# The last layer norm of a two-layer decoder: the first row tile's normalisation is given to ScalarE and GpSimd

## The chip, the cores and the metric

The kernel runs on one core of a Trainium2 chip. The core has five engines that run their own instruction streams and meet at semaphores: TensorE (PE, matmuls), VectorE (DVE), ScalarE (ACT), GpSimd (POOL) and SyncE (SP, which here only issues DMAs). The metric is the device time of one execution in microseconds, lower is better.

## The reference

A decoder of two layers over 256 tokens with 1024 features. The first layer has sparse attention and a dense SwiGLU, the second sliding-window attention and a top-2-of-8 mixture of experts. Each half layer ends in a layer norm, four in all. The change touches the last one alone:

```python
def layer_norm(x, g, b):
    xf = x.astype(jnp.float32)
    mu = xf.mean(-1, keepdims=True)
    var = jnp.square(xf - mu).mean(-1, keepdims=True)
    return ((xf - mu) * lax.rsqrt(var + LN_EPS) * g + b).astype(x.dtype)
...
            ffn = moe_swiglu(h, moe_router[l // 2], moe_w_in[l // 2], moe_w_out[l // 2])
        h = layer_norm(ALPHA * h + ffn, ln_g[l, 1], ln_b[l, 1])
...
    return h
```

## The kernel before

The 256 tokens are two row tiles `tt` of 128 tokens, one token to a partition. `h[:, tt, :]` and `pre[:, tt, :]` hold 1024 columns of each in SBUF, and `lnp[:, 0, :]` and `lnp[:, 1, :]` the norm's gain g and bias b, copied to all partitions.

Some 1,320 us of the program come ahead of the last norm: projections, attention, the dense layer, and the experts, whose weights are streamed from HBM while TensorE multiplies. After the last expert, TensorE's `put_back` adds the experts' rows to what already stands in PSUM (`bank[4 * tt + j]`, 256 columns each, `j` from 0 to 3), first for tile 0, then for tile 1, and raises `e_back` after each of the eight pieces. From there on, the order on each engine is the order in which the code is written, and engines wait for each other by counting semaphores:

- VectorE, for a tile: four `bn_stats`, one a bank; `center`, which merges them (`bn_aggr`, mean and variance in `mv`), adds epsilon (`var_ready`), and writes `pre = (bank - mean) * g` in four pieces; then the inverse of the root. Tile 0 is done whole, up to the inverse (`root_inverted`), before the statistics of tile 1. For tile 1, `scale` writes `h = pre * inverse + b` in two halves (`h_ready`).
- ScalarE: the square root for tile 0 (`root(0)`), then `pre * inverse` of tile 0 in two halves (`pre_scaled`), then `root(1)`, for which VectorE waits in `scale`.
- GpSimd: adds the bias to each half of tile 0 (`first_scaled`). These are its last two instructions.
- SyncE stores the four halves of the output, 256 KB each, in a fixed order on one queue: tile 0's first and second half, then tile 1's. A store that has to wait holds the ones behind it. The program ends when all four have landed:

```python
            for n in range(4):
                if n < 2:
                    sp.wait_ge(first_scaled, n + 1)
                else:
                    sp.wait_ge(h_ready, 12 + n - 1)
                tt, cols = n // 2, slice(512 * (n % 2), 512 * (n % 2) + 512)
                sp.dma_start(out[0, tt * P:tt * P + P, cols], h[:, tt, cols]).then_inc(done, 16)
            sp.wait_ge(done, 16 * 4)
```

`step(...)` issues an instruction and has the engine wait for its end before the next one; `chained(...)` only counts it.

Of the kernel before, what the change touches and what calls it, by code (L numbers as in the profile page):

```python
# [10 lines left out]
ALU = mybir.AluOpType  # L11
ACT = mybir.ActivationFunctionType
X = mybir.AxisListType.X

P = 128
# [144 lines left out]
def decoder_kernel(nc, x, positions, w_in_a, w_out_a, cmp_pos, cmp_w1, cmp_w2, w_kv_shared, w_q_b, w_out_b,  # L160
                   sinks_b, ln_g, ln_b, dense_w_in, dense_w_out, moe_router, moe_w_in, moe_w_out, out):
    ctx = ExitStack()
    with ctx:
        def sb(name, shape, dt=F32):
            return ctx.enter_context(nc.sbuf_tensor(name, shape, dt))

        def sem(name):
            return ctx.enter_context(nc.semaphore(name))
# [34 lines left out]
        sums = sb("sums", [P, 4, 4])  # L203
# [3 lines left out]
        stats = sb("stats", [P, NT, 4, 6])  # L207
        mv = sb("mv", [P, NT, 2])
        std = sb("std", [P, NT, 2])
        lg = sb("lg", [P, 8, NT, NE])  # L210
        selb = sb("selb", [P, NT, NE], BF16)
        top = sb("top", [P, 12, NT, 1])
# [17 lines left out]
        def place(*parts):  # L230

            size = 0
            found = []
            for name, shape, dt in parts:
                found.append(nc.alloc_sbuf_tensor_at(name, shape, dt, offset=base[0]))
                n = 4
                for x_ in shape[1:]:
                    n *= x_
                size = max(size, n)
            base[0] += size  # L240
            return found if len(found) > 1 else found[0]
# [6 lines left out]
        pre = place(("pre", [P, NT, D], F32))  # L248

        lnp, cmp_x = place(("lnp", [P, 2, D], F32), ("cmp_x", [P, 2, CMP_PAIRS, 64], F32))  # L250
# [54 lines left out]
        bank = [psum[:, i, :] for i in range(8)]  # L305
# [18 lines left out]
        dve_step = sem("dve_step")  # L324
# [76 lines left out]
        e_added = sem("e_added")  # L401
        root_inverted = sem("root_inverted")
        pre_scaled = sem("pre_scaled")
        first_scaled = sem("first_scaled")
        done = sem("done")
        zeros_ready = sem("zeros_ready")
# [238 lines left out]
        def _(pool):  # L645
# [98 lines left out]
                                            bass.IndirectOffsetOnAxis(ap=there_i[:, k, tt, :], axis=0)).then_inc(found, 16)  # L744
            for q in range(2):
                cols = slice(512 * q, 512 * q + 512)
                pool.wait_ge(pre_scaled, q + 1)
                pool.tensor_tensor(h[:, 0, cols], pre[:, 0, cols], lnp[:, 1, cols], ALU.add).then_inc(first_scaled, 1)


# [1 line left out]
        def _(act_e):  # L752
            def load_norm(k):
                for part, src in enumerate((ln_g, ln_b)):
                    act_e.dma_start(lnp[:, part, :], src[k // 2, k % 2:k % 2 + 1, :].to_broadcast([P, D]))\
                         .then_inc(ln_landed, 16)
# [3 lines left out]
            def split_weights(upto):  # L760

                upto = min(upto, N_FIRST)
                for n in range(n_round[0], upto):
                    if whole(n):
                        continue
                    act_e.wait_ge(landed[n % RING], 32 * (n // RING + 1))
                    if n >= SPLITS:
                        act_e.wait_ge(used, halves_last(n) + 1)
                    size = size_of(n)
                    act_e.activation(wh[:, n % SPLITS, 0:size], slot_of(n)[:, 0:size], ACT.Copy).then_inc(rounded, 1)  # L770
                n_round[0] = max(n_round[0], upto)

            def turn_h(first, tt):
                for q in range(2):
                    n = 2 * tt + q
                    act_e.wait_ge(turned, first + n + 1)
                    act_e.activation(hTh[:, 4 * q:4 * q + 4, tt * P:tt * P + P],
                                     bank[TBANK[first + n]][:, :].rearrange("p (c n) -> p c n", c=4), ACT.Copy)\
                         .then_inc(high, 1)
# [18 lines left out]
            def stage_part(j, proj, base, nturn, last):  # L798

                kind, _, tt, w = proj[j]  # L800
                if j == len(proj) - NT:
                    act_e.wait_ge(late_done, 1 if proj is PROJ_A else 2)
# [170 lines left out]
            def move_low(first, k):  # L973

                for q in range(2):
                    act_e.wait_ge(lowered, 2 * k + q + 1)
                    act_e.activation(hTl[:, 4 * q:4 * q + 4, 0:P],
                                     bank[TBANK[first + q]][:, :].rearrange("p (c n) -> p c n", c=4), ACT.Copy)\
                         .then_inc(moved_a, 1)

            def permute(tt):

                act_e.wait_ge(h_ready, 8 + 2 * tt + 2)
                act_e.activation(hp[:, tt, :, :], h[:, tt, :].rearrange("p (q c) -> p c q", c=DC), ACT.Copy).then_inc(permuted, 1)

            def turn_part(q, tt):

                act_e.wait_ge(turned, T_H3 + 2 * tt + q + 1)
                act_e.activation(hTf[:, 4 * q:4 * q + 4, tt * P:tt * P + P],
                                 bank[TBANK[T_H3 + 2 * tt + q]][:, :].rearrange("p (c n) -> p c n", c=4), ACT.Copy)\  # L990
                     .then_inc(h_turned_a, 1)

            def norm_part(k, first):

                def root(tt):
                    act_e.wait_ge(var_ready, NT * k + tt + 1)
                    act_e.activation(std[:, tt, 0:1], std[:, tt, 1:2], ACT.Sqrt).then_inc(std_ready, 1)

                root(0)
                if k == 3:  # L1000
                    act_e.wait_ge(root_inverted, 1)
                    for q in range(2):
                        cols = slice(512 * q, 512 * q + 512)
                        act_e.activation(pre[:, 0, cols], pre[:, 0, cols], ACT.Copy, scale=std[:, 0, 1:2]).then_inc(pre_scaled, 1)
                if k < 2:
                    turn_h(first, 0)
                elif k == 2:
                    for q in range(2):
                        turn_part(q, 0)
                root(1)  # L1010
                if k == 2:
                    act_e.wait_ge(tile_routed, 1)
                    act_e.activation(parts[:, 0, :], bank[0][:, 0:P], ACT.Copy).then_inc(parts_a, 1)
                    permute(0)
                    turn_part(0, 1)
                    permute(1)
                    load_norm(k + 1)
                elif k < 2:
                    move_low(first, k)
                    if k:  # L1020
                        split_weights((AT["q_b"], N_FIRST)[k - 1] + 2)
                    turn_h(first, 1)
                    load_norm(k + 1)
# [729 lines left out]
        def _(dve):  # L1753
            n_step = [0]

            def step(ins):

                n_step[0] += 1
                ins.then_inc(dve_step, 1)
                dve.wait_ge(dve_step, n_step[0])  # L1760
# [296 lines left out]
            def chained(ins):  # L2057

                n_step[0] += 1
                ins.then_inc(dve_step, 1)  # L2060
# [5 lines left out]
                                              in1=bank[b][:, :], op0=ALU.mult, op1=ALU.add))  # L2066
                chained(dve.bn_stats(stats[:, tt, half, :], pre[:, tt, cols]))

            def center(tt, sums):

                dve.wait_ge(dve_step, n_step[0])
                step(dve.bn_aggr(mv[:, tt, :], stats[:, tt, 0:len(sums), :].rearrange("p a b -> p (a b)")))
                dve.tensor_scalar(std[:, tt, 1:2], mv[:, tt, 1:2], LN_EPS, None, ALU.add).then_inc(var_ready, 1)
                for at, src in sums:
                    cols = slice(at, at + src.shape[1])
                    chained(dve.scalar_tensor_tensor(out=pre[:, tt, cols], in0=src, scalar=mv[:, tt, 0:1],
                                                     in1=lnp[:, 0, cols], op0=ALU.subtract, op1=ALU.mult))
# [94 lines left out]
            for tt in tiles:  # L2172
                chained(dve.scalar_tensor_tensor(out=tmp[:, tt, :], in0=logits[:, tt, :], scalar=highest[:, tt, 1:2],
                                                 in1=order[:, tt, :], op0=ALU.is_ge, op1=ALU.mult))
            dve.wait_ge(dve_step, n_step[0])
            for tt in tiles:
                chained(dve.scalar_tensor_tensor(out=best[:, tt, :], in0=logits[:, tt, :], scalar=highest[:, tt, 1:2],
                                                 in1=tmp[:, tt, :], op0=ALU.is_gt, op1=ALU.add))
# [9 lines left out]
            for tt in tiles:  # L2188
# [5 lines left out]
                                          in1=sel, op0=ALU.add, op1=ALU.mult))  # L2194
            build_pick()
            step(dve.tensor_tensor(pick2, sel, pick1, ALU.subtract))
            for r in range(1, GROUPS):
# [4 lines left out]
                                          op0=ALU.is_gt, op1=ALU.add))  # L2202
# [96 lines left out]
            for tt in range(NT):  # L2299
                for j in range(4):  # L2300
                    dve.wait_ge(e_back, 4 * tt + j + 1)
                    chained(dve.bn_stats(stats[:, tt, j, :], bank[4 * tt + j][:, 0:256]))
                center(tt, [(256 * j, bank[4 * tt + j][:, 0:256]) for j in range(4)])
                if tt == 0:
                    dve.wait_ge(std_ready, NT * 3 + 1)
                    dve.wait_ge(dve_step, n_step[0])
                    dve.reciprocal(std[:, 0, 1:2], std[:, 0, 0:1]).then_inc(root_inverted, 1)
            scale(3, 1)


# [21 lines left out]
```

## Time and profile before

| | |
|---|---|
| median of 3 runs | 1337.99 us (1337.99 to 1341.41) |
| the profiled execution's own time | 1337.99 us |
| its span, first to last instruction | 1336.2 us |
| busy: TensorE, VectorE, ScalarE, GpSimd | 1309.3, 396.5, 281.2, 75.8 us |
| TensorE's last matmul ends | 1326.3 us |
| last store issued | 1333.74 us |

The span starts with the first instruction and ends with the last, and the execution's own time is 1.79 us longer than it. A start time in a row counts from the span's start. The norm and the stores take the last 11 us.

### The profile page before, as it was taken

Reading aid. Unit: us, or ns where it says so; the run is one execution under the profiler, and the core shown is the slowest. Engines: PE = TensorE matmul, PEld = TensorE weight load, DVE = VectorE, ACT = ScalarE, POOL = GpSimd, SP = SyncE. Lnnn points to the kernel's source line nnn. Section 1 sums busy time; section 2 is a strip of 40 time slices with the busy share of each in tenths; the row PEclk is TensorE's granted clock in tenths of the full one; section 3 lists DMA queues with packets and bytes.
Section 4 is the critical chain, followed back from the end, with each engine's and each line's share of the span. In section 5 each row is a group of like instructions: output and inputs, shape, how many; then the busy total and the mean of one; then the engine's idle time right before and its main releaser. Section 6 shows DMA issues by size and latency. Waiting matters only on the chain.

```text
span 1336.2 us, 31629 instructions
## 1 busy us (share of the span) xinstructions
PE 1309.3 (98%) x14086; PEld 721.6 (54%) x14086; DVE 396.5 (30%) x681; ACT 281.2 (21%) x510; POOL 75.8 (6%) x104
## 2 busy tenths in 40 slices
PE   9998999999999999999999999999999999999996
PEld 6765788888776534533633543443453363354344
DVE  6569666664676411010101101101101010120222
ACT  5456465553455200000010010000000001000001
POOL 2033200000022200000000000000000000000100
PEclk9999999999999999999999999999999999999999
DMA  9680358955542999999999999999999999999992
GB/s 324 196 220 33 126 192 326 332 189 191 158 140 96 379 397 421 417 399 420 418 398 420 419 402 398 419 418 394 420 417 372 420 418 392 408 419 417 418 420 103
DMA packets 115774, 443.16 MB, mean 332 GB/s; under 512 B 11936, under 2 KB 49088, under 8 KB 101312
## 3 DMA queue, kind: packets, MB, share of 16 engines
q1 hardware_dynamic: 108704, 423.39, 81.7%
q10 hardware_dynamic: 5792, 13.63, 2.8%
q0 software_dynamic: 1152, 4.19, 0.8%
q8 instruction: 111, 1.82, 0.6%
q14 instruction: 15, 0.12, 0.0%
HBM read 425.85 MB, written 15.34 MB: 330 GB/s over the span
## 4 chain that ended last, share of the span: by engine, by line
PE 93%; DVE 3%; ACT 2%; SPq 1%; issue 1%; DMA 0%; DVEq 0%; ACTq 0%
PE bank L1731 43%; PE bank L1724 22%; PE bank L1586 6%; PE bank L1142 4%; PE bank L1144 4%; PE bank L1143 4%; PE bank L1589 3%; PE bank L1159 1%; PE bank L1463 1%; PE bank L1424 1%; ACT arena L948 1%; PE bank L1332 1%; PE bank L1172 1%; DMA ring<-in_w_in_a_dram 0%; ACT wh L770 0%
## 5 line engine op out<-in xcount | busy, mean ns | idle before, releaser
L1731 PE MATMUL bank<-ring,arena 128*32 128x448 f32 x2880 | 275.0, 539 | 0.0
L2226 DVE TENSOR_TENSOR arena<-arena,bank 128x448 f32<-128x448 f32 x48 | 26.9, 617 | 727.8 <-PE bank L1731 727.8
L1731 PEld LDWEIGHTS bank<-ring,arena 128*32 128x32 f32 x2880 | 93.4, 110 | 173.9 <-issue 172.6
L1772 DVE TENSOR_TENSOR wl<-ring,wh 128x2048 fp32r<-128x2048 f32 (+1 forms) x54 | 121.7, 2259 | 55.4 <-ACT wh L770 55.1
L1724 PE MATMUL bank<-ring,arena 128*32 128x256 f32 x2304 | 125.8, 379 | 0.0
L1586 PE MATMUL bank<-hT,wh 128*128 128x512 f32 x344 | 121.6, 399 | 0.0
L770 ACT ACTIVATE wh<-ring 128x2048 fp32r<-128x2048 f32 (+1 forms) x56 | 105.5, 1888 | 37.7 <-PE bank L1144 30.7
L1731 PE MATMUL bank<-wls,arena 128*32 128x448 f32 x1152 | 111.2, 539 | 0.0
L1731 PE MATMUL bank<-whs,arena 128*32 128x448 f32 x1152 | 111.2, 539 | 0.0
L1088 ACT ACTIVATE arena<-bank 128x448 f32<-128x448 f32 x48 | 22.6, 544 | 388.8 <-PE bank L1731 388.8
L1724 PEld LDWEIGHTS bank<-ring,arena 128*32 128x32 f32 x2304 | 74.9, 110 | 52.0 <-issue 3.9
L1589 PE MATMUL bank<-hT,wl 128*128 128x256 f32 x344 | 96.6, 281 | 0.0
L1118 ACT ACTIVATE arena<-bank 128x512 f32<-128x512 f32 x7 | 4.2, 597 | 370.8 <-PE bank L1724 370.8
L1731 PEld LDWEIGHTS bank<-wls,arena 128*32 128x32 f32 x1152 | 37.4, 110 | 70.8 <-issue 70.8
L1731 PEld LDWEIGHTS bank<-whs,arena 128*32 128x32 f32 x1152 | 37.4, 110 | 70.8 <-issue 70.8
L1731 PE MATMUL bank<-arena 128*32 128x448 f32 x768 | 75.1, 539 | 0.0
L1586 PEld LDWEIGHTS bank<-hT,wh 128*128 128x128 f32 x344 | 64.6, 188 | 16.0
L1142 PE MATMUL bank<-wh,hT 128*128 128x512 f32 (+1 forms) x176 | 69.1, 393 | 2.9 <-DVE hT L2054 1.2
L1144 PE MATMUL bank<-wl,hT 128*128 128x512 f32 (+1 forms) x176 | 67.0, 381 | 0.0
L1143 PE MATMUL bank<-wh,hT 128*128 128x512 f32 (+1 forms) x176 | 66.9, 380 | 0.0
L1589 PEld LDWEIGHTS bank<-hT,wl 128*128 128x128 f32 x344 | 65.0, 189 | 0.0
L1724 PE MATMUL bank<-whs,arena 128*32 128x256 f32 x1152 | 63.6, 379 | 0.0
(293 smaller groups left out, 1294.6 us busy)
## 6 DMA issues: line engine op xcount, KB each, us to landing
ring<-in_moe_w_in_dram SPq DMA_DIRECT2D x120, 896.0 KB
ring<-in_moe_w_out_dram SPq DMA_DIRECT2D x48, 1024.0 KB
whs<-in_moe_w_in_dram SPq DMA_DIRECT2D x48, 896.0 KB, 17.9
wls<-in_moe_w_in_dram SPq DMA_DIRECT2D x48, 896.0 KB, 18.1
arena<-in_moe_w_in_dram SPq DMA_DIRECT2D x32, 896.0 KB, 16.0
whs<-in_moe_w_out_dram SPq DMA_DIRECT2D x24, 1024.0 KB, 21.3
wls<-in_moe_w_out_dram SPq DMA_DIRECT2D x24, 1024.0 KB, 22.3
ring<-in_dense_w_in_dram SPq DMA_DIRECT2D x22, 1024.0 KB
```

The source lines that it names most:

```text
L770: act_e.activation(wh[:, n % SPLITS, 0:size], slot_of(n)[:, 0:size], ACT.Copy).then_inc(rounded, 1)
L948: ins = act_e.activation(e[:, k * w:k * w + w], score_bank(jobs, i)[:, k * w:k * w + w], ACT.Exp, bias=nb[:, i % 4, k:k + 1], accum_out=su ...
L1088: act_e.activation(act[:, s, :], bank[s][:, 0:BLOCK], ACT.Silu).then_inc(e_silu, 1)
L1142: pe.matmul(out_, lh, rh, start=start, stop=False, skip_group_check=True)
L1143: pe.matmul(out_, ll, rh, start=False, stop=False, skip_group_check=True)
L1144: return pe.matmul(out_, lh, rl, start=False, stop=stop, skip_group_check=True)
L1586: pe.matmul(bank[2 * gu + j], wts[0][:, k, P * j:P * j + P], hT[:, k, :, :].rearrange("p a n -> p (a n)"), start=(k == 0), stop=False, ski ...
L1589: ins = pe.matmul(rest, wts[1][:, k, P * j:P * j + P], hTh[:, k, :], start=False, stop=(k == DC - 1), skip_group_check=True)
L1724: ins = pe.matmul(bank[6 + s // 2][32 * j:32 * j + 32, 256 * (s % 2):256 * (s % 2) + 256], actT[:, half, s, 2 * c + m, :], slot[:, 1024 * ...
L1731: ins = pe.matmul(bank[s + GROUPS * (kind == "u")][32 * j:32 * j + 32, 0:BLOCK], xgT[:, c, 32 * s:32 * s + 32], slot[:, BLOCK * j:BLOCK * ...
L1772: dve.tensor_tensor(wl[:, n % SPLITS, 0:size], slot_of(n)[:, 0:size], wh[:, n % SPLITS, 0:size].bitcast(F32), ALU.subtract).then_inc(split, 1)
L2226: ins = dve.tensor_tensor(act[:, s, :], act[:, s, :], bank[GROUPS + s][:, 0:BLOCK], ALU.mult)
```

## The change

For tile 0, VectorE no longer writes `pre`. It goes from tile 0's epsilon to tile 1's statistics, then inverts tile 0's root and forms a new one-column value, `offset = -mean * inverse`. ScalarE then computes `pre = bank * inverse + offset` from the four banks in PSUM, with a bias operand, in four pieces of 256 columns where it had two of 512 in SBUF. GpSimd multiplies each half of 512 by the gain, waits for that, and adds the bias. SyncE's instructions are as they were.

```diff
@@ GpSimd
             for q in range(2):
                 cols = slice(512 * q, 512 * q + 512)
-                pool.wait_ge(pre_scaled, q + 1)
+                pool.wait_ge(pre_scaled, 2 * q + 2)
+                pool.tensor_tensor(pre[:, 0, cols], pre[:, 0, cols], lnp[:, 0, cols], ALU.mult).then_inc(weighted, 1)
+                pool.wait_ge(weighted, q + 1)
                 pool.tensor_tensor(h[:, 0, cols], pre[:, 0, cols], lnp[:, 1, cols], ALU.add).then_inc(first_scaled, 1)
@@ ScalarE
                 if k == 3:
                     act_e.wait_ge(root_inverted, 1)
-                    for q in range(2):
-                        cols = slice(512 * q, 512 * q + 512)
-                        act_e.activation(pre[:, 0, cols], pre[:, 0, cols], ACT.Copy, scale=std[:, 0, 1:2]).then_inc(pre_scaled, 1)
+                    for j in range(4):
+                        act_e.activation(pre[:, 0, 256 * j:256 * j + 256], bank[j][:, 0:256], ACT.Identity, bias=offset[:, 0:1],
+                                         scale=std[:, 0, 1:2]).then_inc(pre_scaled, 1)
@@ VectorE
-            def center(tt, sums):
+            def center(tt, sums, only_stats=False):
...
                 dve.tensor_scalar(std[:, tt, 1:2], mv[:, tt, 1:2], LN_EPS, None, ALU.add).then_inc(var_ready, 1)
+                if only_stats:
+                    return
...
                     chained(dve.bn_stats(stats[:, tt, j, :], bank[4 * tt + j][:, 0:256]))
-                center(tt, [(256 * j, bank[4 * tt + j][:, 0:256]) for j in range(4)])
-                if tt == 0:
+                if tt:
                     dve.wait_ge(std_ready, NT * 3 + 1)
-                    dve.wait_ge(dve_step, n_step[0])
-                    dve.reciprocal(std[:, 0, 1:2], std[:, 0, 0:1]).then_inc(root_inverted, 1)
+                    step(dve.reciprocal(std[:, 0, 1:2], std[:, 0, 0:1]))
+                    dve.scalar_tensor_tensor(out=offset[:, :], in0=mv[:, 0, 0:1], scalar=-1.0, in1=std[:, 0, 1:2], op0=ALU.mult,
+                                             op1=ALU.mult).then_inc(root_inverted, 1)
+                    center(1, [(256 * j, bank[4 + j][:, 0:256]) for j in range(4)])
+                else:
+                    center(0, [0, 0, 0, 0], only_stats=True)
             scale(3, 1)
```

VectorE's rows at the end of the program, from tile 0's statistics on, before the change (bank names and counts as in the code; "waits" names the semaphores of the instruction):

```order
L2302 BN_STATS stats<-bank 128x6 [waits e_back] x3
L2072 BN_AGGR mv<-stats 128x2 [waits dve_step]
L2073 TENSOR_SCALAR std<-mv 128x1 [waits dve_step]
L2076 SCALAR_TENSOR_TENSOR pre<-bank,mv,lnp 128x256 x4
L2307 RECIPROCAL std<-std 128x1 [waits dve_step,std_ready]
L2302 BN_STATS stats<-bank 128x6 [waits e_back] x4
L2072 BN_AGGR mv<-stats 128x2 [waits dve_step]
L2073 TENSOR_SCALAR std<-mv 128x1 [waits dve_step]
L2076 SCALAR_TENSOR_TENSOR pre<-bank,mv,lnp 128x256 x4
L2082 RECIPROCAL std<-std 128x1 [waits std_ready]
L2085 SCALAR_TENSOR_TENSOR h<-pre,std,lnp 128x512 [waits dve_step]
L2085 SCALAR_TENSOR_TENSOR h<-pre,std,lnp 128x512
```

The same place after the change:

```order
L2308 BN_STATS stats<-bank 128x6 [waits e_back] x3
L2076 BN_AGGR mv<-stats 128x2 [waits dve_step]
L2077 TENSOR_SCALAR std<-mv 128x1 [waits dve_step]
L2308 BN_STATS stats<-bank 128x6 [waits e_back] x4
L2311 RECIPROCAL std<-std 128x1 [waits std_ready]
L2312 SCALAR_TENSOR_TENSOR offset<-mv,std 128x1 [waits dve_step]
L2076 BN_AGGR mv<-stats 128x2 [waits dve_step]
L2077 TENSOR_SCALAR std<-mv 128x1 [waits dve_step]
L2082 SCALAR_TENSOR_TENSOR pre<-bank,mv,lnp 128x256 x4
L2088 RECIPROCAL std<-std 128x1 [waits std_ready]
L2091 SCALAR_TENSOR_TENSOR h<-pre,std,lnp 128x512 [waits dve_step]
L2091 SCALAR_TENSOR_TENSOR h<-pre,std,lnp 128x512
```

The four `pre` pieces of tile 0 are gone, tile 1's `bn_stats` stand directly behind tile 0's epsilon, and the inverse of tile 0's root, with the new `offset`, stands behind them.

GpSimd's last rows before the change, from its last row gathers on:

```order
L736 ISA [waits scattered]
L743 DMA h<-xb,there_i 128x1024 [waits y_stored,e_added]
L743 DMA h<-xb,there_i 128x1024
L743 DMA h<-xb,there_i 128x1024 [waits summed_rows] x2
L748 TENSOR_TENSOR h<-pre,lnp 128x512 [waits pre_scaled] x2
```

And after the change:

```order
L745 DMA h<-xb,there_i 128x1024 [waits summed_rows] x2
L750 TENSOR_TENSOR pre<-pre,lnp 128x512 [waits pre_scaled]
L752 TENSOR_TENSOR h<-pre,lnp 128x512 [waits weighted]
L750 TENSOR_TENSOR pre<-pre,lnp 128x512 [waits pre_scaled]
L752 TENSOR_TENSOR h<-pre,lnp 128x512 [waits weighted]
```

Two instructions of 512 columns became four of the same form, in two pairs, in each of which the second waits for the first.

## Rows read from the trace of the kernel before

**Rows 1.** The chain of work that ended last, from 1318 us: start us, us, what

```profile
1323.42 1.66 PE bank L1694 x24
1325.08 1.44 DVE stats L2302 x4
...
1326.99 1.58 DVE pre L2076 x4
...
1328.66 0.16 DVE std L2307
1328.82 1.33 DVE stats L2302 x4
...
1330.18 0.28 DVE mv L2072
...
1330.63 1.57 DVE pre L2076 x4
1332.20 0.08 DVE std L2082
```

**Rows 2.** VectorE's timeline at the end: start us, us, instruction, [idle before]

```profile
1326.84 0.15 DVE L2073 TENSOR_SCALAR std<-mv 128x1 f32<-128x1 f32 x1
...
1332.30 1.41 DVE L2085 SCALAR_TENSOR_TENSOR h<-pre,std,lnp 128x512 f32<-128x512 f32 x2
```

**Rows 3.** ScalarE's timeline at the end

```profile
1322.89 0.84 ACT L1111 ACTIVATE arena<-bank,gate_slot 128x256 f32<-128x256 f32 x2 [32.62 <-PE bank L1724]
...
1327.03 0.20 ACT L997 ACTIVATE std<-std 128x1 f32<-128x1 f32 x1 [1.27 <-DVE std L2073]
1328.86 1.33 ACT L1004 ACTIVATE pre<-pre,std 128x512 f32<-128x512 f32 x2 [1.63 <-DVE std L2307]
```

**Rows 4.** ScalarE's line L1004: count, duration ns min/median/max, first and last start

```profile
L1004 ACT ACTIVATE pre<-pre,std x2: 705/713/721, 1328.9 to 1329.5; 128x512 f32<-128x512 f32 x2
```

**Rows 5.** GpSimd's timeline: the end, and three small instructions early in the program

```profile
10.06 0.77 POOL L689 TENSOR_TENSOR quads<-quads,ident 128x8 f32<-128x8 f32 x3
...
1329.66 2.48 POOL L748 TENSOR_TENSOR h<-pre,lnp 128x512 f32<-128x512 f32 x2 [65.01 <-ACT pre L1004]
```

**Rows 6.** GpSimd's groups by shape: count | busy us, mean ns | idle before

```profile
L716 POOL TENSOR_SCALAR arena<-arena,rg 128x256 f32<-128x256 f32 x48 | 46.5, 984 | 267.4 <-DVE rg L2015 230.1 <-DVE rg L2020 37.3
L725 POOL TENSOR_SCALAR pre<-h 128x2048 f32<-128x2048 f32 x1 | 5.4, 5367 | 27.3 <-DVE h L2085 27.3
...
L748 POOL TENSOR_TENSOR h<-pre,lnp 128x512 f32<-128x512 f32 x2 | 2.5, 1262 | 65.0 <-ACT pre L1004 65.0
...
L689 POOL TENSOR_TENSOR quads<-quads,ident 128x8 f32<-128x8 f32 x3 | 0.6, 206 | 0.2
```

**Rows 7.** SyncE's queue: the last two of the four stores

```profile
1333.08 0.33 SPq L640 DMA_DIRECT2D out_dram<-h  x1
...
1333.74 0.33 SPq L640 DMA_DIRECT2D out_dram<-h  x1
```

**Rows 8.** DMA from 1331 to 1337 us in 40 slices of 0.15 us

```profile
GB/s 0 0 0 0 0 246 341 410 382 328 41 55 0 123 382 410 396 341 96 178 396 382 369 369 369 423 396 355 260 0 0 0 0 0 0 0 0 0 0 0
```

**Rows 9.** GpSimd's L716 and VectorE's L1780 side by side, 98 to 102 us

```profile
98.08 1.22 DVE L1780 TENSOR_TENSOR wl<-ring,wh 128x1024 fp32r<-128x1024 f32 x1
...
98.25 1.83 POOL L716 TENSOR_SCALAR arena<-arena,rg 128x256 f32<-128x256 f32 x1 [1.32 <-DVE rg L2020]
...
99.81 1.21 DVE L1780 TENSOR_TENSOR wl<-ring,wh 128x1024 fp32r<-128x1024 f32 x1
...
100.07 1.75 POOL L716 TENSOR_SCALAR arena<-arena,rg 128x256 f32<-128x256 f32 x1
```

**Rows 10.** Durations over all executions of L716, L1780 and L2076 (256 columns)

```profile
L716 POOL TENSOR_SCALAR arena<-arena,rg x48: 919/926/1834, 74.6 to 414.4; 128x256 f32<-128x256 f32 x48
...
L1780 DVE TENSOR_TENSOR wl<-ring,wh x4: 1211/1216/1443, 98.1 to 135.8; 128x1024 fp32r<-128x1024 f32 x4
...
L2076 DVE SCALAR_TENSOR_TENSOR pre<-bank,mv,lnp x8: 472/474/475, 1326.9 to 1331.7; 128x256 f32<-128x256 f32 x8
```

More of the change, by code:

```diff
@@ L209, in decoder_kernel @@
         std = sb("std", [P, NT, 2])
+        offset = sb("offset", [P, 1])
         lg = sb("lg", [P, 8, NT, NE])
@@ L403, in decoder_kernel @@
         pre_scaled = sem("pre_scaled")
+        weighted = sem("weighted")
         first_scaled = sem("first_scaled")
```

## The prediction

> **What bounds the kernel now.** I read the chain of work that ended last first, then the timelines of VectorE, ScalarE, GpSimd and the store queue over the last 14 us. TensorE is busy for 1309.3 of 1336.2 us, and nothing of its work is touched. Its last pieces for tile 0 are ready at 1325.08, and from there the chain is VectorE's alone [rows 1]: the reader is to see that tile 0's `pre` (1.58 us) and inverse (0.16) stand in it ahead of tile 1's statistics (1.33), its merge (0.28) and its own `pre` (1.57). VectorE ends with the two halves of `h` of tile 1, from 1332.30 for 1.41 us, so at 1333.71 [rows 2]. GpSimd had finished its two additions at 1329.66 + 2.48 = 1332.14 [rows 5], 1.57 us earlier, and they cost nothing. The last store is issued at 1333.74 and the span ends at 1336.2, which is 2.46 us after it [rows 7].
>
> **The change part by part.** All is summed from the profiled execution: span 1336.2, its own time 1337.99, the same as the median, so 1.79 us are added to a span.
>
> VectorE. Tile 0's epsilon is written at 1326.84 + 0.15 = 1326.99, as before [rows 2]. Tile 1's four `bn_stats` follow, for which TensorE (last matmul 1326.3) is ready: 1328.32. The inverse costs 0.16 [rows 1], and its root is there since 1327.23 [rows 3]: 1328.48. `offset` is not in the trace. Below it lies the 0.08 of an overlapped one-column instruction (the second inverse) [rows 1], above it the 0.28 of the merge. It is nearest to the one-column addition of epsilon (0.15) [rows 2], with a wait of 0.02 for its input as between the merge and the epsilon: 1328.65. Merge 0.02 + 0.28, epsilon 0.02 + 0.15, `pre` of tile 1 1.57, inverse 0.08, give 1330.77. The two halves of `h` start at 1330.79 and end at 1332.20, which is 1.51 us earlier than before, if nothing holds them.
>
> ScalarE. It starts 0.04 us after the inverse before (1328.82 to 1328.86) [rows 1, 3], so now at 1328.69. Its four pieces read PSUM with a scale and write SBUF, as L1111 does: two take 0.84, one alone 0.47, so 0.37 each beside the next [rows 3]. Two are done at 1329.53 and four at 1330.27, so `root(1)` ends at about 1330.47, 0.3 us before VectorE asks for it. The bias operand has no row. I take nothing for it; at 0.1 each it would take 0.2 from GpSimd's start. The upper bound, half of a 512-column piece from SBUF that does not overlap (0.36) [rows 4], is no more than the 0.37 taken.
>
> GpSimd. Before, it started 0.08 us after ScalarE's first half (1328.86 + 0.72 to 1329.66) [rows 3 to 5]. Now it starts at about 1329.62, practically unmoved. Here it has four instructions where it had two. The addition is 1.262 us [rows 6], and two in a row take 2.48, so 0.03 are lapped [rows 5]. A multiplication of two tensors stands nowhere in the trace. From below it is the addition's 1.262. From above, the line through the two multiplications by one factor, 0.92 us for 256 columns [rows 10] and 5.37 for 2048 [rows 6], gives 1.55 for 512. I take 1.262, since form, shape and operands are those of L748. A dependent pair has a gap: three dependent additions of 0.206 take 0.77, so 0.08 each [rows 5, 6]. Without a disturbance the four run from 1329.62 to 1330.88, 1330.96 to 1332.22, 1332.19 to 1333.45 and 1333.53 to 1334.79. So GpSimd, not VectorE, is last, and 2.65 us later than it was.
>
> The meeting of the two. Before, VectorE's `h` halves came after GpSimd was done. Now they start at 1330.79, in the middle. Both of their inputs lie in SBUF, and the trace shows what such an instruction does to GpSimd: L716 takes 0.92 alone, but 1.83 when it starts 0.17 us behind L1780, and ends 0.77 behind it; the next one the same way 1.75 [rows 9, 10]. It worked as if it had started 0.13 to 0.15 us before L1780 ended. L2076, with one input in PSUM, took 472 to 475 ns whether GpSimd worked or not [rows 10], so it doesn't matter. Applied here: the second GpSimd instruction (ready 1330.96) can work from 1331.54 - 0.13 = 1331.41 if it comes between the two halves, or from 1332.20 - 0.13 = 1332.07 if both go ahead. In the latter case the rest is 1333.33, 1334.56, then 1334.64 to 1335.90. In the former, the second half of `h` waits for GpSimd (to 1332.54 at most), ends at 1333.29, and holds the third instruction to 1333.16: the end is 1335.76. Both ways cost about 1.0 to 1.1 us. I take 1335.85 as GpSimd's end; below it is 1334.79 (no meeting).
>
> The Trainium skill bears on this, in sentences that the sum does without. "SBUF — State Buffer", section "Who interferes with whom", says that a VectorE instruction with two SBUF inputs contends with a GpSimd instruction that reads SBUF, and that the later one blocks until the other has finished. The trace agrees for GpSimd behind VectorE, to 0.15 us [rows 9]. It disagrees the other way round: L1780 started at 99.81, while L716 ran to 100.07, and took its plain 1.21 [rows 9, 10]. By the rule in full the four would end at about 1336.2, and the kernel at 1341.9, the top of the forecast's own range.
>
> Stores. SyncE's order puts tile 1's two stores behind tile 0's second half, which GpSimd now ends last. VectorE's 1.51 us therefore buy nothing: its results wait in the queue. The second, third and fourth store are issued together at 1335.88, and 768 KB go out at once. Before, from the issue of the third (1333.08) to the end of the span lay 3.12 us [rows 7], in which the bytes of the last two moved back to back in 10 slices of 0.15, so 0.75 each [rows 8]. One more behind them gives 3.12 + 0.73 = 3.85. The lower bound is that only the issues count: 0.35 + 0.35 + 2.46 = 3.16. I take the upper, since there is no gap between the last two though they were issued 0.66 apart [rows 7, 8].
>
> Sum: 1335.88 + 3.85 = 1339.73 of span, + 1.79 = 1341.5; with a part of the doubt in the tail, **1341.4 us**, 3.4 us or 0.25% above the median before.
>
> **The rivals.**
> (a) No meeting: the `h` halves and GpSimd do not disturb each other, which the 1.83 us of L716 speak against [rows 9], and only the difference in instruction (these have a third, one-column operand) speaks for. 1334.79 + 0.03 + 3.85 + 1.79 = 1340.5; with the short tail 1339.8.
> (b) The other side, slower by more than the bound below: GpSimd's multiplication is dearer than its addition. Its place is L750, its price at the upper bound 2 x 0.29 = 0.58 us, so GpSimd ends at 1336.43 and the kernel at 1342.1. For it speaks that one-factor multiplications cost 2.6 ns a column (5367 for 2048), and the two-input addition 2.1 (from 8 to 512 columns, 206 to 1262) [rows 6]. Against it, those are another form, with a factor that is the same for all columns. It decides from 0.50 us for both together on: 1.51 us an instruction. The skill's "GPSIMD Engine Reference", section "Elementwise — side-by-side cycle accounting", puts the cost of a two-input instruction down to reading both operands, not to arithmetic; by that rule it would be 1.26 and this rival is out. No row here shows it.
> (c) Faster: VectorE sets the end, 1332.20 + 0.04 + 2.46 + 1.79 = 1336.5. It would need GpSimd to finish by 1331.9, four instructions in 2.3 us, where four of 1.262 take 5.05 [rows 6]. Even then it is a gain of 1.5 us, inside the bound.
>
> **How the numbers follow.** 0.3%, 4.0 us, is about what a measurement of this kernel tells from no change: the runs before range over 3.4 us. So the lines are 1334.0 and 1342.0. Forecast 0.55 (its own range 1340.8 to 1341.9), (a) 0.17, (b) 0.20, (c) 0.02, and 0.06 for something in the 1,320 us ahead, such as shifted addresses, where a third counts as slower. Faster 0.02, within 0.3% 0.76, slower 0.22. The range goes from (a) with the short tail, 1339.8, to just above (b), 1342.5.
>
> **What the changed profile would show.** VectorE's last instruction ending at 1332.2 to 1333.3, earlier than before; GpSimd with four instructions of 1.26, the second or third stretched to 1.7 to 2.4, the last ending near 1335.9; three stores issued 0.35 apart behind it; the chain naming GpSimd and the stores. Wrong would be: a GpSimd end before 1334 or after 1336.5, stores that move at less than 0.7 us each, ScalarE's `root(1)` later than 1330.8 with VectorE waiting for it, or a start of the norm (1325.08) that has moved.

## The result and the profile after

The changed kernel takes 1342.1 us (median of 12 runs, 1341.05 to 1343.08) against 1338.56 us (12 runs, 1337.95 to 1341.41): ratio 1.0022, 95% interval 1.0015 to 1.0029. The medians differ by 3.54 us, and the interval stands for 2.0 to 3.9 us. So the slowing is clear of the noise, and it lies below the 0.3% at which I had drawn the line.

Its profiled execution took 1342.67 us with a span of 1340.9 us, and in it the norm started 1.35 us later than in the one of before (1326.43 against 1325.08 us [rows 1]). Those 1.35 us arise long before the norm: a table load of ScalarE that starts at 453.24 us in the trace of before starts at 454.59 here. Over the ten profiles of this study the norm starts between 1324.13 and 1326.50, with the kernel before and the two versions built on it at 1324.97 to 1325.74, inside that range. I take it for scatter. All that follows is read from the **tail**: from the first `bn_stats` of the last norm to the end of the span. Before it is 1336.2 - 1325.08 = 11.12 us, after it is 1340.9 - 1326.43 = 14.47: 3.35 us more, and the medians differ by 3.54.

Of the changed kernel, VectorE's timeline at the end (start us, us, instruction), which answers to [rows 1, 2]:

```profile
1326.43 1.43 DVE L2308 BATCH_NORM_STATS2 stats<-bank 128x6 f32<-128x256 f32 x4 [1.69 <-PE bank L1698]
...
1328.26 1.41 DVE L2308 BATCH_NORM_STATS2 stats<-bank 128x6 f32<-128x256 f32 x4
1329.59 0.14 DVE L2311 RECIPROCAL std<-std 128x1 f32<-128x1 f32 x1
1329.77 0.16 DVE L2312 SCALAR_TENSOR_TENSOR offset<-mv,std 128x1 f32<-128x1 f32 x1
...
1332.02 0.16 DVE L2088 RECIPROCAL std<-std 128x1 f32<-128x1 f32 x1 [0.17 <-ACT std L1001]
1332.22 2.42 DVE L2091 SCALAR_TENSOR_TENSOR h<-pre,std,lnp 128x512 f32<-128x512 f32 x2
```

Its ScalarE and GpSimd timelines, to read beside [rows 3, 5], and its last three stores in SyncE's queue, beside [rows 7]:

```profile
1329.96 1.93 ACT L1007 ACTIVATE pre<-bank,offset,std 128x256 f32<-128x256 f32 x4 [1.39 <-DVE offset L2312]
1331.78 0.21 ACT L1001 ACTIVATE std<-std 128x1 f32<-128x1 f32 x1
...
1331.07 1.27 POOL L750 TENSOR_TENSOR pre<-pre,lnp 128x512 f32<-128x512 f32 x1 [64.74 <-ACT pre L1007]
1332.42 1.67 POOL L752 TENSOR_TENSOR h<-pre,lnp 128x512 f32<-128x512 f32 x1
1334.05 1.71 POOL L750 TENSOR_TENSOR pre<-pre,lnp 128x512 f32<-128x512 f32 x1
1335.84 1.26 POOL L752 TENSOR_TENSOR h<-pre,lnp 128x512 f32<-128x512 f32 x1
...
1337.13 1.31 SPq L642 DMA_DIRECT2D out_dram<-h  x3
```

What the DMA engines moved from 1332 to 1342 us, in 40 slices of 0.25 us:

```profile
GB/s 0 0 0 0 0 0 0 0 0 0 0 57 377 385 230 33 0 0 0 0 0 0 0 49 369 385 352 377 393 377 393 393 58 0 0 0 0 0 0 0
```

The reader is to see three things. VectorE's two `h` instructions took 2.42 us for 1.41, and still ended at 1334.64, 8.21 us into the tail (8.63 before). GpSimd's four end at 1337.10, 10.67 us into the tail (7.06 before), the middle two stretched to 1.67 and 1.71. And three stores go out together right behind it, with 1340.9 - 1337.10 = 3.80 us from GpSimd's end to the end of the span. In the DMA row their bytes are one block without a gap, some 0.7 us a store.

### The profile page after: what moved, and what is told of

It reads as the page before. It is cut to its first block, busy times and chain, and to the rows that moved or that the text cites. A ratio compares the mean times of both kernels' runs of the same rounds, so it can differ in the third digit from the quotient of the medians.

```text
span 1340.9 us, 31629 instructions
## 1 busy us (share of the span) xinstructions
PE 1309.5 (98%) x14086; PEld 722.0 (54%) x14086; DVE 396.1 (30%) x678; ACT 281.5 (21%) x512; POOL 79.0 (6%) x106
## 3 DMA queue, kind: packets, MB, share of 16 engines
q10 hardware_dynamic: 5792, 13.63, 2.8%
## 4 chain that ended last, share of the span: by engine, by line
PE 92%; DVE 3%; ACT 2%; SPq 1%; issue 1%; DMA 1%; POOL 0%; POOLq 0%; ACTq 0%; DVEq 0%
PE bank L1735 43%; PE bank L1728 22%; PE bank L1590 6%; PE bank L1146 4%; PE bank L1148 4%; PE bank L1147 4%; PE bank L1593 3%; PE bank L1163 1%; PE bank L1467 1%; PE bank L1428 1%; ACT arena L952 1%; PE bank L1336 1%; DMA ring<-in_w_in_a_dram 1%; PE bank L1176 1%; DVE pre L2043 0%
```

## The experiments

The times of these kernels scatter by some us a run, so each verdict rests on the tail, and the ratio to the kernel before, run beside it, stands next to it. The tail comes from one profile of each version; the same rows in different profiles agree to a few hundredths of a us. The ratios alone would not put the versions in order: their intervals overlap.

**The order of the stores.** Only SyncE's order is changed:

```diff
-            for n in range(4):
+            for n in (0, 2, 3, 1):
```

> The changed kernel with one edit: SyncE issues the stores in the order tile 0 first half, tile 1 both halves, tile 0 second half. Read as the tail: from the first bn_stats of the last norm to the end of the span, 11.12 us in the profile before and 14.47 in the profile after. My theory: GpSimd's last instruction ends 10.67 us into the tail as in the changed kernel, but only one store is then left, which took 2.46 us before, so the tail is 13.2 us and the time 1.3 us below the changed kernel's. Rival, that the stores move freely and only GpSimd's end counts: GpSimd's end plus 3.8 us again, tail 14.5.

Measured: tail 1338.3 - 1325.16 = 13.14 us, ratio to the kernel before 1.0015 (1.0004 to 1.0026). In its GpSimd timeline and SyncE's queue the last addition ends at 1335.82, the same 10.66 us into the tail, and one store stands behind it:

```profile
1325.16 1.43 DVE L2308 BATCH_NORM_STATS2 stats<-bank 128x6 f32<-128x256 f32 x4 [1.69 <-PE bank L1698]
...
1334.56 1.26 POOL L752 TENSOR_TENSOR h<-pre,lnp 128x512 f32<-128x512 f32 x1
...
1335.85 0.33 SPq L642 DMA_DIRECT2D out_dram<-h  x1
```

So 1.33 us of the loss are the stores of tile 1's two finished halves, which waited behind the store of an unfinished one. The rival, 14.5, is out.

**Tile 1's `pre` kept in PSUM**, so that VectorE's `h` instructions have one input in SBUF:

```diff
-                    chained(dve.scalar_tensor_tensor(out=pre[:, tt, cols], in0=src, scalar=mv[:, tt, 0:1],
+                    chained(dve.scalar_tensor_tensor(out=src if in_psum else pre[:, tt, cols], in0=src, scalar=mv[:, tt, 0:1],
...
+                        dve.scalar_tensor_tensor(out=h[:, tt, cols].rearrange(two, j=2), in0=psum[:, 4 + 2 * q:6 + 2 * q, 0:256],
+                                                 scalar=std[:, tt, 1:2], in1=lnp[:, 1, cols].rearrange(two, j=2),
+                                                 op0=ALU.mult, op1=ALU.add).then_inc(h_ready, 1)
...
```

> The changed kernel with one edit: VectorE leaves tile 1's pre in the four PSUM banks in place of SBUF, so that its two h instructions have one input in SBUF and not two. My theory, that the two engines hold each other up where both of VectorE's inputs are in SBUF: all four GpSimd instructions take 1.26 to 1.27 us (1.67 and 1.71 in the middle of the changed kernel), VectorE's second h instruction about 0.75 (1.75), GpSimd ends 9.8 us into the tail, and the tail is 13.6 us (14.47 in the changed kernel). Rival, that the multiplication or the wait inside a pair costs the time: the middle two stay at 1.67 to 1.71, tail 14.5.

Measured: tail 1340.0 - 1326.37 = 13.63 us, ratio 1.0026 (1.0016 to 1.0037). The timelines of VectorE and GpSimd:

```profile
1326.37 1.42 DVE L2314 BATCH_NORM_STATS2 stats<-bank 128x6 f32<-128x256 f32 x4 [1.69 <-PE bank L1698]
...
1332.16 1.41 DVE L2093 SCALAR_TENSOR_TENSOR h<-bank,std,lnp 128x512 f32<-128x512 f32 x2
...
1331.01 1.27 POOL L750 TENSOR_TENSOR pre<-pre,lnp 128x512 f32<-128x512 f32 x1 [64.89 <-ACT pre L1007]
1332.36 1.27 POOL L752 TENSOR_TENSOR h<-pre,lnp 128x512 f32<-128x512 f32 x1
1333.58 1.26 POOL L750 TENSOR_TENSOR pre<-pre,lnp 128x512 f32<-128x512 f32 x1
1334.92 1.26 POOL L752 TENSOR_TENSOR h<-pre,lnp 128x512 f32<-128x512 f32 x1
```

All four are back at 1.26 to 1.27, VectorE's pair at 1.41, though they lie beside each other as before. The stretching, 0.85 us in sum, goes away when one of VectorE's two inputs leaves SBUF, so it came from both engines working on SBUF while VectorE had two inputs there. The same rows settle the multiplication: it costs what the addition costs. VectorE's four `pre` pieces took 1.66 us into PSUM and 1.65 into SBUF, so the edit cost nothing there.

**Both edits.**

> The edits of the store order and of pre in PSUM together. My theory: they add, GpSimd ends 9.8 us into the tail and one store of 2.46 us follows, tail 12.3 us, still 1.2 us above the kernel before (11.12), because four GpSimd instructions of 1.26 us are the path. Rival, that the queue and the meeting are the whole loss: tail 11.1 or less.

Measured: tail 1336.4 - 1324.13 = 12.27 us, ratio 1.0014 (0.9999 to 1.0028). The norm's start and GpSimd's last addition:

```profile
1324.13 1.43 DVE L2314 BATCH_NORM_STATS2 stats<-bank 128x6 f32<-128x256 f32 x4 [1.69 <-PE bank L1698]
...
1332.69 1.26 POOL L752 TENSOR_TENSOR h<-pre,lnp 128x512 f32<-128x512 f32 x1
```

GpSimd ends 9.82 us into the tail, and 2.45 us follow. The two edits add up. What is left, 1.15 us over the kernel before, is GpSimd's four instructions in a row, with one store behind them.

**Without the multiplications.** The two `tensor_tensor(..., ALU.mult)` and the waits on `weighted` are taken out of the changed kernel; tile 0 then lacks the gain.

> The changed kernel without GpSimd's two multiplications: tile 0 is not multiplied by the gain, so this leaves out part of the norm. It shows what the other parts of the change are worth without the added GpSimd work. My theory: GpSimd's second addition still meets VectorE's first h instruction and ends 7.7 us into the tail, three stores then move together, and the tail is 11.5 us, no better than before (11.12), though VectorE is done by 8.3. Rival, that VectorE sets the end once GpSimd's extra work is gone: VectorE at 7.2, tail 9.7.

Measured: tail 1337.7 - 1326.18 = 11.52 us, ratio 1.0002 (0.9990 to 1.0014). The norm's start and GpSimd's two additions:

```profile
1326.18 1.42 DVE L2306 BATCH_NORM_STATS2 stats<-bank 128x6 f32<-128x256 f32 x4 [1.69 <-PE bank L1696]
...
1330.82 3.02 POOL L750 TENSOR_TENSOR h<-pre,lnp 128x512 f32<-128x512 f32 x2 [66.38 <-ACT pre L1005]
```

The additions take 3.02 us for 2.48, since they still meet VectorE's `h`. GpSimd ends at 1333.84, 7.66 us into the tail (7.06 before), and 3.86 us follow, for three stores that go out together. Even with the added work gone, nothing is gained.

**The added GpSimd work alone.** The kernel before, where GpSimd multiplies by the gain a second time; VectorE and ScalarE are untouched:

```diff
...
+                pool.tensor_tensor(pre[:, 0, cols], pre[:, 0, cols], lnp[:, 0, cols], ALU.mult).then_inc(weighted, 1)
+                pool.wait_ge(weighted, q + 1)
                 pool.tensor_tensor(h[:, 0, cols], pre[:, 0, cols], lnp[:, 1, cols], ALU.add).then_inc(first_scaled, 1)
```

> The kernel before with GpSimd's two multiplications added and nothing moved on VectorE and ScalarE, so tile 0 is multiplied by the gain twice. It prices the added GpSimd work without the reordering. My theory: GpSimd's last two instructions and VectorE's two h instructions take turns, GpSimd ends at 10.1 us into the tail, VectorE at 10.7, and the tail is 13.6 to 14.0 us, against 14.47 for the whole change and 11.12 for the kernel before: the reordering itself gives nothing back, the added GpSimd work is the loss. Rival, that the loss comes from moving the work to PSUM and the offset: tail below 12.

Measured: tail 1338.9 - 1324.97 = 13.93 us, ratio 1.0019 (1.0007 to 1.0031). VectorE's `h` pair and GpSimd's last two instructions:

```profile
1324.97 1.43 DVE L2305 BATCH_NORM_STATS2 stats<-bank 128x6 f32<-128x256 f32 x4 [1.69 <-PE bank L1697]
...
1332.18 3.41 DVE L2088 SCALAR_TENSOR_TENSOR h<-pre,std,lnp 128x512 f32<-128x512 f32 x2
...
1332.12 1.26 POOL L749 TENSOR_TENSOR pre<-pre,lnp 128x512 f32<-128x512 f32 x1
1333.45 1.59 POOL L751 TENSOR_TENSOR h<-pre,lnp 128x512 f32<-128x512 f32 x1
```

GpSimd ends 10.07 us into the tail, VectorE 10.62. Here VectorE came second and paid: 3.41 us for 1.41. The added work alone costs 2.81 us of tail; the whole change costs 3.35, so moving the instructions about gave nothing back and took another half microsecond. That half is mainly the meeting, which fell on GpSimd's chain there (0.86 us of stretching) more than here (0.33).

**ScalarE's pieces.** The changed kernel, with the four pieces in four forms; its output lacks parts of the norm:

```diff
...
+                        how = ((ACT.Copy, {"scale": std[:, 0, 1:2]}), (ACT.Identity, {"scale": std[:, 0, 1:2]}),
+                               (ACT.Identity, {"bias": offset[:, 0:1]}),
+                               (ACT.Identity, {"bias": offset[:, 0:1], "scale": std[:, 0, 1:2]}))[j]
...
```

> The changed kernel with ScalarE's four pieces of tile 0 in four forms, so its output leaves out parts of the norm: Copy with a scale, Identity with a scale, Identity with a bias, Identity with both. In the changed kernel all four have both and take 0.56 us, one each 0.46; I had forecast 0.47 and 0.37 from a Copy with a scale. Theory, that the bias operand costs it: the first two 0.47, the last two 0.56. Rival, that Identity costs it against Copy: the first 0.47, the other three 0.56.

Measured, in the profile of its only execution: ScalarE's first two pieces together, then the third and the fourth, and below them the norm's start and GpSimd's last addition.

```profile
1330.04 0.84 ACT L1010 ACTIVATE pre<-bank,std 128x256 f32<-128x256 f32 x2 [1.39 <-DVE offset L2314]
1330.77 0.47 ACT L1010 ACTIVATE pre<-bank,offset 128x256 f32<-128x256 f32 x1
1331.12 0.57 ACT L1010 ACTIVATE pre<-bank,offset,std 128x256 f32<-128x256 f32 x1
...
1326.50 1.43 DVE L2310 BATCH_NORM_STATS2 stats<-bank 128x6 f32<-128x256 f32 x4 [1.69 <-PE bank L1700]
...
1335.65 1.26 POOL L752 TENSOR_TENSOR h<-pre,lnp 128x512 f32<-128x512 f32 x1
```

Both theories fall. Identity costs what Copy costs, and a bias from an SBUF column costs what a scale from one costs (0.47 each, 0.35 to 0.37 beside the next). Having both costs 0.10 more: it is the second column operand that is paid for. What a piece with none takes, no run here shows. GpSimd ends 10.41 us into the tail here, and the tail is 1340.7 - 1326.50 = 14.20 us, 0.27 less than the changed kernel's.

**A version that shares tile 0.** GpSimd has three instructions, VectorE forms `pre` for tile 0's second half with one instruction over two banks, the inverse and the offset stand between tile 1's `bn_stats`, the `pre` of tile 1 stays in PSUM, and the stores alternate between the tiles:

```diff
...
-                pool.wait_ge(pre_scaled, 2 * q + 2)
-                pool.tensor_tensor(pre[:, 0, cols], pre[:, 0, cols], lnp[:, 0, cols], ALU.mult).then_inc(weighted, 1)
-                pool.wait_ge(weighted, q + 1)
+                pool.wait_ge(pre_scaled, q + 2)
+                if q == 0:
+                    pool.tensor_tensor(pre[:, 0, cols], pre[:, 0, cols], lnp[:, 0, cols], ALU.mult).then_inc(weighted, 1)
+                    pool.wait_ge(weighted, 1)
...
+            dve.scalar_tensor_tensor(out=pre[:, 0, 512:1024].rearrange(two, j=2), in0=psum[:, 2:4, 0:256], scalar=mv[:, 0, 0:1],
+                                     in1=lnp[:, 0, 512:1024].rearrange(two, j=2), op0=ALU.subtract, op1=ALU.mult)\
+               .then_inc(root_inverted, 1)
...
```

> A version meant to beat both kernels: tile 0's first half goes the new way (ScalarE from PSUM, GpSimd multiplies and adds), its second half the old way (VectorE subtracts and multiplies, ScalarE scales, GpSimd adds), the inverse and the offset stand between tile 1's second and third bn_stats, tile 1's pre stays in PSUM, and the stores go out as tile 0 first, tile 1 first, tile 0 second, tile 1 second half. GpSimd has three instructions. My theory: GpSimd ends 7.9 us into the tail, VectorE 7.8 (8.63 before), but three stores then move close together, so the tail is 11.0 us against 11.12 before: no gain to be measured. Rival, that the engines' end decides: 7.9 + 2.5, tail 10.4.

Measured: tail 1337.5 - 1325.89 = 11.61 us, ratio 1.0002 (0.9993 to 1.0011). GpSimd ended 7.81 us and VectorE 7.60 us into the tail, as forecast and both earlier than VectorE's 8.63 before, but the tail is half a microsecond longer. Its DMA row (1332 to 1338 us in slices of 0.15) and its queue show why:

```profile
GB/s 0 0 0 0 0 0 0 0 0 328 410 382 341 328 328 423 341 423 328 355 437 396 396 369 369 410 382 219 27 27 14 14 0 0 0 0 0 0 0 0
...
1332.51 2.04 SPq L642 DMA_DIRECT2D out_dram<-h  x4
```

From 1333.35 on the DMA engines move the whole megabyte without a gap until 1336.2, with some stragglers behind. The first store went out 6.62 us into the tail; before it was 5.87 (1330.95). All four are now one block of 2.85 us, and it starts later. I had counted three stores as the block and forecast 11.0: a miss, by the first store and the stragglers.

**The kernel before, with wider instructions.** This version takes from the last one the `pre` instruction over two banks, now for both tiles. Tile 0's inverse stands behind the first half of its `pre`, and ScalarE waits for each half by itself. GpSimd is as in the kernel before.

```diff
...
-                center(tt, [(256 * j, bank[4 * tt + j][:, 0:256]) for j in range(4)])
+                for q in range(2):
+                    cols, at = slice(512 * q, 512 * q + 512), 4 * tt + 2 * q
+                    ins = dve.scalar_tensor_tensor(out=pre[:, tt, cols].rearrange(two, j=2), in0=psum[:, at:at + 2, 0:256],
+                                                   scalar=mv[:, tt, 0:1], in1=lnp[:, 0, cols].rearrange(two, j=2),
+                                                   op0=ALU.subtract, op1=ALU.mult)
...
```

> The kernel before with two edits on VectorE, none on GpSimd: the four subtract-and-multiply pieces of 256 columns of each tile become two instructions of 512 that read two banks each (0.65 us beside the next, against 0.79 for two pieces), and tile 0's inverse stands behind its first half. My theory, that in the kernel before the end is set by VectorE and that its instructions' fixed cost can be saved: VectorE ends 8.1 us into the tail (8.63), the first store goes out at 4.9 (5.87), the stores are spread enough that only the last counts, tail 10.6 us (11.12). Rival, that the stores' bytes set the end: 11.1. In time, 0.5 us is too little to be told from no change: ratio within 0.1% of 1.

Measured: tail 1336.3 - 1325.74 = 10.56 us, ratio 0.9991 (0.9982 to 1.0000). VectorE's timeline:

```profile
1325.74 1.43 DVE L2304 BATCH_NORM_STATS2 stats<-bank 128x6 f32<-128x256 f32 x4 [1.69 <-PE bank L1694]
...
1328.49 0.73 DVE L2309 SCALAR_TENSOR_TENSOR pre<-bank,mv,lnp 128x512 f32<-128x512 f32 x1
...
1330.96 1.40 DVE L2309 SCALAR_TENSOR_TENSOR pre<-bank,mv,lnp 128x512 f32<-128x512 f32 x2
...
1332.46 1.41 DVE L2087 SCALAR_TENSOR_TENSOR h<-pre,std,lnp 128x512 f32<-128x512 f32 x2
```

VectorE ends at 1333.87, 8.13 us into the tail, and 2.43 us behind it the span ends, as behind one store (2.45 with both edits). The rival, 11.1, is out. It is the one version whose tail is below that of the kernel before, by 0.56 us; its time cannot be told from no change.

## Why the prediction was right

The forecast was 1341.4 us, 3.4 above before; the medians differ by 3.54 and the tails by 3.35. The absolute time, 1342.1, is just above the forecast's own range (up to 1341.9) and is by chance the figure of rival (b). Of the 0.7 us between them, 0.57 is that the kernel before came out at 1338.56 in this comparison and not at 1337.99. The steps:

- **GpSimd becomes last.** Right. Its end was forecast 10.77 us into the tail (1335.85 - 1325.08; 10.68 by the course that came about, 1335.76) and came at 10.67. It started 0.10 us later than forecast (4.64 us in, for 4.54): ScalarE's first two pieces took 0.18 longer, since one costs 0.46 beside the next and not 0.37, and VectorE was ready 0.08 earlier. The price of the bias operand was taken as nothing, and 0.1 each was named as its doubt. With VectorE's earliness the longer pieces also made VectorE wait 0.17 us for `root(1)`. The prediction has 0.3 us of slack there; its own sum leaves 0.22, since VectorE asks at 1330.69, ahead of the 0.08 of the inverse.
- **That the end fits to 0.1 us is in part luck.** In the version with four forms the first two pieces take the 0.84 us that were forecast. There `h` starts 5.54 us in, where 5.71 was forecast (1330.79 - 1325.08), and GpSimd ends at 10.41. So VectorE's small instructions had been summed 0.17 us too long, ScalarE's pieces too short, and the two errors hid each other.
- **The multiplication.** Taken as the addition's 1.262; 1.27 and 1.26 where nothing disturbs it. Rival (b) is out.
- **The meeting.** Forecast 1.0 to 1.1 us, measured 0.85 (13.63 against 14.47 in the tail, and 1.67 + 1.71 against 2 x 1.26). Of the two courses it was the former: GpSimd came between VectorE's halves. VectorE's first half ended at 1332.97 and GpSimd's second instruction ran as if from 1332.83, 0.14 before that, the distance that the early rows showed [rows 9]. Rival (a) is out, shown by taking the second SBUF input away.
- **The stores.** Forecast 3.88 us from GpSimd's end to the end of the span, measured 3.80, and 3.82 without the meeting. Where VectorE ends half a microsecond behind GpSimd (without the multiplications, and with the added work alone) it is 3.86. With one store left behind it, it is 2.48. The upper value was nearer: the bytes of the three stores count, and not only their issues. The sum took 0.73 us for the third store where its own rows give 0.75; here it is some 0.7.
- **VectorE's 1.51 us buy nothing.** Right. It kept 0.42 of them, and they waited in the queue.

Of the signs named for being wrong, two came up by the clock, through the 1.35 us ahead of the norm: its start had moved, and GpSimd ended after 1336.5. Counted from the norm's start GpSimd's end stands at 1335.75 on the forecast's scale. `root(1)` made VectorE wait, but ended 5.56 us in, within the 5.72 that were named (1330.8 - 1325.08).

Against the trace, the rule of the Trainium skill ("SBUF — State Buffer", section "Who interferes with whom") holds in kind in both directions: GpSimd waited for VectorE, and VectorE's second half took 1.75 us for 0.75 behind GpSimd. By it alone GpSimd would have ended at about 1336.2, 11.1 us into the tail, and it ended at 10.67, though it started 0.10 late: what waits gets going 0.14 to 0.20 us before the other's record ends.

The prediction had read from L1780 at 99.81 that VectorE is not held behind GpSimd. The trace of before has a row that says otherwise, the longest L1780, which [rows 10] shows only as the maximum of 1443 ns:

```profile
131.10 1.83 POOL L716 TENSOR_SCALAR arena<-arena,rg 128x256 f32<-128x256 f32 x2
...
132.12 1.44 DVE L1780 TENSOR_TENSOR wl<-ring,wh 128x1024 fp32r<-128x1024 f32 x1
```

It started 0.11 us behind the second of these L716 (from 132.01) and took 1.44 us for 1.21, as if held until 132.35, some 0.6 before that L716 ended. At 99.81 only 0.26 of an L716 was left. So the hold seems to end well before a short GpSimd instruction does, but 0.20 before GpSimd's addition ended in the changed kernel. What sets this is open.

The chance of 0.22 for slower by over 0.3% was not idle, as the interval's upper end, 1.0029, comes close.

## What to carry to other kernels

Work handed to an engine that was idle costs nothing only until that engine ends last: sum its whole chain first, with the gap between dependent instructions, before counting what the relieved engine gains. Look at what stands in the queue behind its result; a fixed order of stores turns one late piece into three late ones, and near the end the bytes of the last megabyte are a bound of their own (2.85 us in the version that shares tile 0). And where two engines are made to overlap, look at where their inputs lie: an operand left in PSUM took the 0.85 us of stretching away, and the `pre` pieces cost the same (1.66 us for 1.65).

## What the hardware showed that I had not expected

- A ScalarE instruction of 128x256 from PSUM takes 0.47 us with a scale from a column or a bias from a column, and 0.56 to 0.57 with both.
- One VectorE instruction that subtracts and multiplies over 512 columns in two PSUM banks takes 0.73 us, 0.65 to 0.67 beside the next, against 0.79 for two of 256 (1.57 for four [rows 1]).
- Who pays when VectorE and GpSimd meet differed with who came first. In the changed kernel `h` started at 1332.22 and GpSimd's instruction 0.20 us behind it, and they shared it (1.0 us for VectorE, 0.85 for GpSimd). With the added work alone GpSimd's third instruction started at 1332.12 and `h` 0.06 behind it, and VectorE paid 2.0 us and GpSimd 0.3.
